# Expert results weighed as they are stored, added onto x2 by the gathers, last tile written out in slot order

## The reference, cut to what matters

```python
x = x + hybrid_mixer(rms_norm(x, norm1_g[l]), ...)          # this sum is called x2 here
xn = rms_norm(x, norm2_g[l])
# router: one of 4 groups, in it the best 2 of 4 experts (16 experts, 512 wide);
# combine[token, expert] = the two picks' shares, summing to the group's weight
for e in range(N_EXPERTS):
    h = silu(xt @ w_gate[e]) * (xt @ w_up[e])
    y = y + combine[:, e:e + 1] * (h @ w_down[e])
return rms_norm(x + y, final_norm_g)
```

## Time and profile before

| | |
|---|---|
| median of the runs | 788.62 us |
| the profiled execution's own time | 789.02 us |
| its span in the profile | 787.3 us |
| last matmul of the experts starts | 767.43 us |
| first gather issued, last one issued | 758.13, 768.05 us |
| last output store issued | 784.30 us |

### The profile page before, as it was taken

How to read it: one execution, slowest core, us unless ns; L and a number is a source line. 1 busy time by engine, 2 the same in 40 slices (tenths; PEclk the granted TensorE clock), 3 DMA queues, 4 the chain that set the end, 5 groups by cost and what they waited for, 6 DMA issues and landing times.

```text
span 787.3 us, 10839 instructions
## 1 busy us (share of the span) xinstructions
PE 764.9 (97%) x3739; PEld 621.8 (79%) x3739; DVE 492.3 (63%) x702; ACT 450.5 (57%) x590; POOL 209.3 (27%) x124
## 2 busy tenths in 40 slices
PE   7999999999999999999999999999999999999994
PEld 4788777777787888888888788878778888888782
DVE  5704476585743302322022669999999998999888
ACT  5244657566744232323321556787878888888862
POOL 3644433232332444434442532000000000000033
PEclk9999999999999999999999999999999999999998
DMA  8569999792222262332328438999999999999965
GB/s 300 183 213 381 370 337 393 268 342 75 69 66 81 81 214 87 100 107 81 107 97 282 161 131 285 408 409 409 409 409 409 410 409 410 409 409 341 398 251 202
DMA packets 134318, 206.74 MB, mean 263 GB/s; under 512 B 10813, under 2 KB 65669, under 8 KB 134278
## 3 DMA queue, kind: packets, MB, share of 16 engines
q1 hardware_dynamic: 126084, 188.80, 65.7%
q10 hardware_dynamic: 5890, 9.04, 3.1%
q0 software_dynamic: 2304, 8.39, 2.8%
HBM read 157.95 MB, written 48.25 MB: 262 GB/s over the span
## 4 chain that ended last, share of the span: by engine, by line
PE 85%; DVE 6%; ACTq 2%; DMA 2%; POOL 2%; ACT 1%; issue 1%; DVEq 0%; SPq 0%; POOLq 0%
PE ps L1052 25%; PE ps L1054 24%; PE ps L1053 24%; DVE w_lo L389 3%; PE ps L1342 2%; PE ps L1146 1%; PE ps L1174 1%; PE ps L1157 1%; PE ps L1295 1%; POOL raw_mg L656 1%; PE ps L1269 1%; DMA x<-in_x 1%; PE ps L1349 1%; ACTq L877 1%; DMA raw_mg<-slots,slot_idx 1%
## 5 line engine op out<-in xcount | busy, mean ns | idle before, releaser
L383 POOL TENSOR_TENSOR w_lo<-raw,w_hi 128x1024 fp32r<-128x1024 f32 x72 | 174.1, 2422 | 250.4 <-ACT w_hi L371 250.4
L371 ACT ACTIVATE w_hi<-raw 128x1024 fp32r<-128x1024 f32 x73 | 76.8, 1057 | 195.4 <-PE ps L1054 168.0
L1052 PE MATMUL ps<-xn_hi,w_hi 128*128 128x512 f32 x352 | 140.6, 399 | 0.0
L1054 PE MATMUL ps<-xn_hi,w_lo 128*128 128x512 f32 x352 | 137.2, 390 | 0.0
L1053 PE MATMUL ps<-xn_lo,w_hi 128*128 128x512 f32 x352 | 137.1, 390 | 0.0
L1052 PE MATMUL ps<-w_hi,xT_hi 128*128 128x512 f32 (+1 forms) x248 | 97.0, 391 | 2.2 <-DVE w_lo L389 2.2
L1054 PE MATMUL ps<-w_hi,xT_lo 128*128 128x512 f32 (+1 forms) x248 | 95.1, 384 | 0.0
L1053 PE MATMUL ps<-w_lo,xT_hi 128*128 128x512 f32 (+1 forms) x248 | 94.9, 383 | 0.0
L656 POOL DMA_INDIRECT raw_mg<-slots,slot_idx x7 | 7.8, 1113 | 280.4 <-DMA slots<-y_tile 278.5
L1052 PEld LDWEIGHTS ps<-xn_hi,w_hi 128*128 128x128 f32 x352 | 66.1, 188 | 16.2 <-issue 2.0
L1053 PEld LDWEIGHTS ps<-xn_lo,w_hi 128*128 128x128 f32 x352 | 66.1, 188 | 14.1 <-issue 1.0
(11 more groups left out here) (311 smaller groups left out, 1475.1 us busy)
## 6 DMA issues: line engine op xcount, KB each, us to landing
slots<-raw SPq DMA_DIRECT2D x65, 512.0 KB, 7.0
raw<-in_w_in SPq DMA_DIRECT2D x52, 512.0 KB, 4.0
raw_mg<-in_exp_w_down SPq DMA_DIRECT2D x35, 512.0 KB, 11.0
raw<-in_exp_w_gate SPq DMA_DIRECT2D x29, 512.0 KB, 11.3
raw_a<-in_exp_w_gate SPq DMA_DIRECT2D x26, 512.0 KB, 10.6
raw_c<-in_exp_w_up SPq DMA_DIRECT2D x24, 512.0 KB, 11.8
raw_mg<-in_exp_w_up SPq DMA_DIRECT2D x22, 512.0 KB, 11.9
raw<-in_exp_w_up SPq DMA_DIRECT2D x15, 512.0 KB, 11.8
```

What stands on the lines that cost most here:

```text
L371: nc.scalar.activation(w_hi[:, b % HI_SLOTS, :], raw_buf(b), ACT.Copy)\
L383: eng.tensor_tensor(w_lo[:, b % HI_SLOTS, :], raw_buf(b), w_hi[:, b % HI_SLOTS, :].bitcast(F32), ALU.subtract)\
L1052: pe.matmul(dst, hi_l, hi_r, start=start, stop=False)
L1054: return pe.matmul(dst, lo_l, hi_r, start=False, stop=stop)
```

## The change

- A second DRAM tensor, `info`, holds for every slot four words: output row, weight, the slot of the token's other pick, and a zero. POOL fills it with defaults, writes the picks' entries with 8 indirect scatters of 16 bytes a row, and reads it back as `slot_info`. VectorE makes the weights early for that (`share_of_picks`, `combine_weights`, `info_rows`).
- `y_part` multiplies by the slot's weight while it copies (scale from `slot_info`), and waits for `info_in`. One buffer (`y_home`) takes the place of three. The first tile's result is copied in the next tile's pass, at `r == 2`.
- x2 rows of the tokens that have a pick in the last tile are scattered into `last_x`, by slot, and loaded back as `z_home`. `last_rows_out` makes the indices; rows with no such pick have an index out of bounds and are left out.
- The gathers add in the transfer (`compute_op=ADD`) onto `x_rows`, which holds x2. First come four that need no result of tile 14 (`gather_order` puts picks in that tile second), after the copy of tile 14's result; then one that adds the other picks of the last tile's tokens onto `z_home`, after that result has landed in DRAM; then, when the first four have landed, the other four.
- The last tile's result is weighed and added onto `z_home` straight from PSUM (`z_sum`), squared, normed and written by slot: its rows go to their tokens' places with an indirect scatter. The one-hot matrices, their matmuls and the sums on VectorE are gone.
- All outputs are written by POOL with indirect scatters; rows that the last tile writes are left out of the other four by an index out of bounds. SP writes none.

```diff
+            def add_picked(rows, idx, landed_in):
+                pool.indirect_dma_start(rows, None, slots, bass.IndirectOffsetOnAxis(ap=idx, axis=0),
+                                        compute_op=ALU.add).then_inc(landed_in, 16)
+            pool.wait_ge(S["y_act"], n_stop + PAIRED)
+            pool.wait_ge(S["y_stored"], n_stop * 16 + 16 * (PAIRED - 1))
+            pool.wait_ge(S["info_in"], 16)
+            pool.tensor_copy(last_info[:, :], info_words[:, bass.ds(last_block * 4, 4)])
+            pool.wait_ge(S["routed"], NT + 3)
+            for t in range(NT):
+                add_picked(x_rows[:, t, :], slot_idx[:, 2 * t:2 * t + 1], S["early_in"])
+            pool.wait_ge(S["z_in"], 16)
+            pool.wait_ge(S["consts_pool"], 21)
             pool.wait_ge(S["before_last_stored"], 16)
+            add_picked(z_home, last_info[:, 2:3], S["z_in"])
+            pool.wait_ge(S["early_in"], 16 * NT)
             for t in range(NT):
-                gather(0, y_lo(t), t)
-                gather(1, y_hi(t), t)
-            for t in range(NT):
-                pool.wait_ge(S["y_stat"], t + 1)
-                pool.tensor_tensor(stat[:, 7, t:t + 1], stat[:, 6, t:t + 1], minus_half[:, :], ALU.pow)
+                add_picked(x_rows[:, t, :], slot_idx[:, 2 * t + 1:2 * t + 2], rows_in[t])
+            power(0)
+            power(1)
+            power(2)
+            rows_out(0)
+            power(3)
+            rows_out(1)
+            power(NT)
+            rows_out(2)
+            pool.wait_ge(S["z_norm"], 2)
+            pool.indirect_dma_start(out[0], bass.IndirectOffsetOnAxis(ap=last_info[:, 0:1], axis=0), z_weighed, None,
+                                    bounds_check=TOK - 1, oob_is_err=False).then_inc(S["y_out"], 16)
+            rows_out(3)
...
+                act.wait_ge(S["info_in"], 16)
+                act.wait_ge(S["y_stored"], at.y_count)
+                act.activation(y_home, ps[:, 5:7, :].rearrange("p a n -> p (a n)"), ACT.Copy,
+                               scale=info_words[:, bass.ds(block * 4 + 1, 1)].bitcast(F32)).then_inc(S["y_act"], 1)
...
+            y_square(0)
+            y_square(1)
+            y_square(2)
+            z_square(0)
+            y_square(3)
+            z_square(1)
+            act.activation(z_weighed[:, 0:512], z_weighed[:, 0:512], ACT.Copy, scale=stat[:, 4, 3:4])
...
+            y_mean(0, 1)
+            y_normed(0)
+            y_mean(1, 2)
+            dve.wait_ge(S["z_in"], 32)
+            z_sum(0)
+            z_sum(1)
+            y_mean(2, 3)
+            y_normed(1)
+            z_weigh(0)
+            y_mean(3, 5)
+            z_weigh(1)
+            dve.wait_ge(S["y_sq"], NT + 2)
+            link(dve.tensor_tensor(stat[:, 4, 2:3], stat[:, 4, 0:1], stat[:, 4, 1:2], ALU.add))
+            dve.tensor_scalar(stat[:, 4, 2:3], stat[:, 4, 2:3], 1.0 / D, EPS, ALU.mult, ALU.add)
+            y_normed(2)
+            dve.wait_ge(S["y_rstd"], NT + 1)
+            dve.wait_ge(S["z_weighed"], 2)
+            dve.tensor_scalar(z_weighed[:, 512:], z_weighed[:, 512:], stat[:, 4, 3:4], None, ALU.mult)
+            y_normed(3)
```

More of the change, by code:

```diff
@@ new lines, in _ @@
+            pool.dma_start(info_words, info.rearrange("(p b) n -> p (b n)", p=P)).then_inc(S["info_in"], 16)
+            pool.wait_ge(S["routed"], NT + 2)
+            for t in range(NT):
+                pool.indirect_dma_start(last_x, bass.IndirectOffsetOnAxis(ap=last_places[:, t:t + 1], axis=0),
+                                        x_rows[:, t, :], None, bounds_check=P - 1, oob_is_err=False)\
+                    .then_inc(S["last_x_out"], 16)
+            pool.wait_ge(S["last_x_out"], 16 * NT)
@@ L973, in _, with tile @@
                     xT_hi_part(2, first_hi)
-            def tile(at, block=None, tile_index=None):
+            FIRST, SECOND = 1, 2
+            def tile(at, block=None, tile_index=None, count=None):
                 i = at.i
@@ L979, in tile @@
                     split_hi_loop(at, r + AHEAD + 1)
+                    if r == 2 and count == SECOND:
+                        y_part(loop_block(1, PER_TILE), at_odd(0), 0)
                     if r == 3:
@@ L989, in tile @@
                         xT_hi_part(i + 2)
-                y_part(loop_block(i, PER_TILE), at, block)
+                if count != FIRST:
+                    y_part(loop_block(i, PER_TILE), at, block)
             def block_of(tile_index):
@@ L996, in _ @@
             split_hi_loop(at_odd(0), AHEAD)
[L997 to L998 removed]
+            tile(at_odd(0), 0, count=FIRST)
+            tile(at_even(1), PER_EXPERT, count=SECOND)
             tile(at_odd(1), 2 * PER_EXPERT)
@@ new lines, in _, with gather_order @@
+            at_first, at_second = top_slot[:, :, 1], top_slot[:, :, 0]
+            swap, apart, before_rows = four(13), four(14), four(15)
+            def gather_order(before):
+                dve.tensor_scalar(before_rows[:, 0:1], block_table[:, bass.ds(before, 1)], float(P), None, ALU.mult)
+                link(dve.tensor_scalar(before_rows[:, 1:2], block_table[:, bass.ds(before, 1)], float(P), float(P),
+                                       ALU.mult, ALU.add))
+                link(dve.tensor_scalar(swap, at_first, before_rows[:, 0:1], None, ALU.is_gt))
+                link(dve.scalar_tensor_tensor(out=swap, in0=at_first, scalar=before_rows[:, 1:2], in1=swap,
@@ L2112, in _, with z_sum, z_weigh @@
-            for c in range(2):
-                last_norm(3, slice(512 * c, 512 * (c + 1)))
+            def z_sum(c):
+                at = slice(512 * c, 512 * (c + 1))
+                dve.wait_ge(S["w_used"], loop_block(tiles, 3 + c))
+                dve.scalar_tensor_tensor(out=z_home[:, at], in0=ps[:, 5 + c, :], scalar=last_info[:, 1:2].bitcast(F32),
+                                         in1=z_home[:, at], op0=ALU.mult, op1=ALU.add).then_inc(S["z_sum"], 1)
+            def z_weigh(c):
+                at = slice(512 * c, 512 * (c + 1))
+                dve.wait_ge(S["z_sum"], c + 1)
+                dve.tensor_tensor(z_weighed[:, at], z_home[:, at], gf_rows[:, at], ALU.mult)\
+                   .then_inc(S["z_weighed"], 1)
```

312 lines of the change are left out of this document (139 added, 173 removed).

## The result

| | before | after |
|---|---|---|
| median of the runs | 788.96 us (787.97 to 789.51) | 803.94 us (803.34 to 804.47) |
| span in the profile | 787.3 us | 802.4 us |
| last matmul of the experts starts | 767.43 us | 770.83 us |
| first gather issued | 758.13 us | 758.96 us |
| last output issued | 784.30 us | 797.41 us |

The change makes the kernel slower by 1.9%: the ratio is 1.0191, with an interval of 1.0173 to 1.0209. Forecast were 798.6 us and a range up to 802.5: the direction was right, the size was 5.3 us short, and the time lies outside the range.

What follows compares the result with a forecast made beforehand. TensorE, 85% of the span, bounds the kernel; only the end could be won. An early start, handed back by the wait, doubled transfers and POOL's output list gave span 797.3 + 1.7 - 0.4 = 798.6 us, range 788.5 to 802.5.

Steps and rivals of the forecast that it cites:

- the adding gather: Gathers at the end: adding reads the target row too, so 2.8 us a transfer instead of 1.57.
- the wait hands back the start: Second four gathers wait for the first four; POOL idle from 761.8 to 770.3, giving back the 2.8 us won.
- the output list: POOL's five powers and five scatters at the end: last landing 784.9, last scatter begins 793.4, span ends 797.3 us.
- the holds: POOL's powers and scatters held by VectorE instructions with two SBUF inputs; span 797.3 us, without any holding 795.2.
- TensorE notices nothing until about 515.6 ... I take 0: Expert stage: the info round trip stays inside the split blocks in hand; bounds 0 and 2.4 us, 0 taken.
- The cover: Expert stage: three split blocks in hand, less one split and the copy, keep TensorE fed until about 515.6 us.
- a case of one in four: Expert stage: the round trip of info comes late, by up to 2.4 us; the rows favour it about one time in four.
- VectorE's +0.6 and +0.8 us: Weight instructions at 487.7 us and behind hid (492.98) add this to VectorE, but cost nothing; 1.4 us without the lead.
- the lead of three blocks: Expert stage: TensorE works from three split blocks ahead (AHEAD), a block about 1.4 us, covering VectorE's added instructions.
- the start and the first transfers: POOL copies last_info (some 0.5 us), first add at 755.3; the first four land from 761.5 to 769.9 us.
- the 1.7 taken over: Step from span to time: execution 1.7 us longer than its span, as in the kernel before.
- the early start: End: the first add is issued at 755.3 us instead of 758.13, 2.8 us won.

Runs made afterwards that it cites:

- e1: Changed kernel with all nine adding gathers made plain, the wait between the two sets kept: 794.75 us, ratio 1.0079.
- e3: Changed kernel, still adding, but the second four gathers go onto four other buffers without waiting for the first four: 803.06 us.
- e5: Changed kernel with SP storing the groups in token order, the last tile's rows, power and scaling left out: 799.33 us.
- e12: Changed kernel, everything computed: plain picks' gathers, VectorE sums, later weighed copy, last tile's rows written ahead of groups 2 and 3: 798.35 us.
- e7: Changed kernel with the four groups scaled on ScalarE instead of VectorE, final_norm_g left out for them: 804.69 us.
- e9: Changed kernel with the weighed copy of the first tile's result moved from r == 2 to r == 4, nothing left out: 802.1 us.
- e8: Changed kernel with the first tile's result copied unweighed in its own pass and VectorE's weight instructions removed: 800.58 us.
- e6: Changed kernel with the first four gathers also waiting until tile 14's result has landed in DRAM: 808.52 us.
- e11: Kernel before, with only the early start: plain second-pick gathers issued at the copy of tile 14's result: 789.8 us, ratio 1.0016.
- four edits: Changed kernel with plain gathers, no wait between sets, first copy unweighed, no VectorE weights, and outputs stored by SP: 782.02 us.

## Why the prediction was right in kind and wrong in size

**Right: the adding gather.** 2.8 us were taken for a transfer and 2.5 to 2.8 came out, against the plain row's 1.57. e1 shows the difference with all else equal, 9.2 us of time. Why an addition costs that much no run separates; the row of `x_rows` that must be read too fits the 1.9 times per packet. (The Trainium skill, *Collectives: The Full Stack*, "The bandwidth ceiling: the fold count and why AG ≠ RS ≠ AR", states for a ring of several cores that a reducing transfer's two source reads halve the rate. By that rule an estimate for this gather is 2 x 1.57 = 3.14 us; this case's trace has 2.5 to 2.8 us, a ratio of 1.6 to 1.8, a little under it.)

**Right: the wait hands back the start.** The stretch from the fourth landing to the last was forecast at 15.0 us and took 14.8 (774.57 to 789.36). POOL's idle time was 4.3 us and not 8 to 9, because its own longer issues filled the rest. e3 adds that taking the wait away gives back only 0.5 to 2.3 us, since the transfers are full without it.

**Right in sum, partly by luck: the output list.** From the last landing to the end of the span 12.4 us were forecast, and it took 13.0. The parts differ. The last scatter began 8.0 us behind the last landing for 8.5 and landed 3.2 us after its issue for 3.5, but the span ended 1.8 us behind that landing, where 0.4 had been taken over from the kernel before. That 0.4 belongs to an end with a store of SP (0.5 in e5); where POOL's scatter is last it is 1.8 us in after, in e1 and in e12 alike. Of the powers one was held, not most. What sets the length is the series of mean, power, scaling and scatter with every power and scatter in POOL's one list; e5 shows it, and e7 leaves open how much of it the holds are.

**Wrong: "TensorE notices nothing until about 515.6 ... I take 0".** The round trip ended at 518.9, beyond the 512 to 518 allowed. The first scatter began 0.8 us after the weights were ready, which had no term; eight scatters beside a full load queue and VectorE's splits were issued in 1.42 us on the mean and not 0.95 to 1.38, the last landed 5.98 us after its issue, above the 5.7 of the earlier trace rows, and the read took 4.93. The rows 8 came from a stretch with 124 GB/s (452 to 472 us) and 278 GB/s (472 to 484 us), this one runs at 409; that this is why they were short is likely and not tested. The cover itself was sized well: the copy came 3.43 us late and TensorE lost 2.23 of it. That is close to the upper bound of 2.4, which the text had held for a case of one in four. e9 puts the price at 1.8 us of time.

**Wrong: VectorE's +0.6 and +0.8 us, "covers it: nothing".** TensorE paid 0.24 and 0.47 us of it in gaps at 491 and 496 us. The forecast had taken the lead of three blocks from the steady stage. That it is still being built at the start of the experts would explain the gaps; no run tests it, e8 shows only that they go with the instructions.

**Mis-sized: the start and the first transfers.** POOL's first add comes 1.1 us behind the end of the copy and not 0.5, and the first four need 15.6 us from the first issue to the fourth landing for 14.6: an adding issue takes 1.54 us undisturbed, 1.67 to 2.50 here, where 0.95 to 1.3 had been put in silently. Whether the issues are the cause of that 1.0 us is not shown. The store of tile 14's result beside them is not: e6 starts behind it and needs 16.4 us.

The span error of 5.1 us is the sum: first add at 758.96 for 755.3, +3.7 (the copy ends 3.1 late by `info`, the gaps and some 0.45 us that differ before 450 us without the change; the start 0.6), the first four +1.0, the second four -0.2, the tail +0.6. The execution was 2.1 us longer than its span for the 1.7 taken over, and the median 0.5 below it for 0.4, which makes the 5.3. The step that failed is the expert stage, held in the forecast to cost nothing ("I take 0"): the round trip and the weights took TensorE 2.9 us, and with them the whole of the 2.8 us for which the early start was counted. e11 shows that an early start was worth nothing in the old arrangement either, in the order of rows tried there, since VectorE's line set its end.

The range was also added up wrong. Its own bounds, 3.1 us a transfer (8 x 0.3 = 2.4 us more) and 2.4 us for `info`, give 798.6 + 2.4 + 2.4 = 803.4 us and not 802; the measured 803.94 is half a microsecond above that.

What stays open: the cost of the holds, the long runs of e6, and why an adding issue takes 1.54 us. A full queue is an unlikely reason, since the four issues of the second set read 1.54 to 1.55 us each although the DMA engines are only 58% busy during the first two (774.6 to 778.0 us).

## What to carry to other kernels

Before an accumulation is put into a transfer, look at how full the DMA engines are. Here, where the plain gathers already filled them to 0.91, it made each one 1.6 to 1.8 times as long, 0.9 to 1.3 us more, while the VectorE sum that it replaces costs 1.28 us; whether it pays where they have room no run shows. A new round trip through DRAM should be costed by the worst rows of a busy stage, and its consumer put as late in the engine's list as the data allow: putting it 3.7 us later was worth 1.8 us of time in the median. And before a start is moved earlier, look at which engine's line has no gap to the end; if it has none, as here, an earlier landing is worth nothing.

## What the hardware showed beyond the forecast

An adding indirect gather costs POOL 1.54 us to issue where the plain one costs 0.94 (after and e1, same lines, same rows), so it slows the issuing engine as well as the queue. In the adding stretches the DMA engines read as 97 to 105% busy at 182 to 200 GB/s of rows: the profile counts nearly the same bytes as for plain gathers (2.26 and 2.16 MB), and 1.9 times the engine time per packet. A program whose last act is an indirect scatter of POOL ended 1.8 us behind its landing (after, e1, e12), one that ends with SP's stores 0.4 to 0.5 us (before, e5). And single removals undercounted: four edits, -18.4 us when taken one by one, gave -21.9 together.
